# First modulation group in two parts: shift and scale ahead of the first sublayer, its gate third in gated jobs 3 to 10

## The reference

```python
def sublayer_input(x, g, mod_j):
    shift, scale, gate = mod_j[:, 0], mod_j[:, 1], mod_j[:, 2]
    h = rmsnorm(x, g) * (1 + scale[:, None, :]) + shift[:, None, :]
    return h, (1 + gate)[:, None, :]

def swiglu(h, w_gu, w_down):
    g, u = jnp.split(h @ w_gu, 2, axis=-1)
    return (jax.nn.silu(g) * u) @ w_down

    c_act = jax.nn.silu(c)
        mod = (c_act @ mod_w[layer] + mod_b[layer]).reshape(B, N_SUB, 3, D_MODEL)
        h, g = sublayer_input(x, norm_g[layer, 0], mod[:, 0])
        x = x + MACARON_W * g * swiglu(h, ffn_w_gu[layer, 0], ffn_w_down[layer, 0])
```

## Time and profile before

| | |
|---|---|
| median of 3 runs | 2380.91 us (2377.79 to 2382.84) |
| profiled execution | 2378.58 us |
| its span | 2377.0 us |
| granted TensorE clock, mean | 0.962 of full speed |
| PE busy | 2221.3 us, 93% |
| DVE busy | 1644.3 us, 69% |
| ACT busy | 1218.7 us, 51% |
| POOL busy | 327.2 us, 14% |
| DMA, mean | 224 GB/s |

### The profile page before, as it was taken

The page is one execution under the profiler, slowest core; times in us unless marked ns, Lnnn a source line. Parts: engine busy times, 40 slices in busy tenths (PEclk is TensorE's granted clock), DMA queues, the critical chain, the costliest instruction groups (busy, mean ns, idle before and its releaser), DMA issues.

```text
span 2377.0 us, 37520 instructions
## 1 busy us (share of the span) xinstructions
PE 2221.3 (93%) x14452; PEld 2031.1 (85%) x14452; DVE 1644.3 (69%) x1961; ACT 1218.7 (51%) x1911; POOL 327.2 (14%) x482
## 2 busy tenths in 40 slices
PE   2999999999999996999998999998998799998998
PEld 2998887998899795899886998987987798877987
DVE  6767764767776776776787776796766776665654
ACT  2544445544554465653464554556545554575543
POOL 0111000111121103021101120400210221000210
PEclk9999999999999998999999999999999899999999
DMA  8788883698897872797765678513788378442553
GB/s 335 249 300 292 273 295 109 239 315 288 262 322 258 310 220 72 225 324 266 259 225 189 197 262 287 174 53 99 256 288 246 91 269 282 148 135 71 180 201 106
DMA packets 296577, 532.97 MB, mean 224 GB/s; under 512 B 10097, under 2 KB 187644, under 8 KB 296444
## 3 DMA queue, kind: packets, MB, share of 16 engines
q1 hardware_dynamic: 263452, 358.05, 46.2%
q0 software_dynamic: 32992, 173.09, 20.4%
HBM read 530.00 MB, written 1.11 MB: 223 GB/s over the span
## 4 chain that ended last, share of the span: by engine, by line
PE 82%; DVE 7%; ACT 5%; issue 3%; DMA 3%; SPq 0%; POOL 0%; DVEq 0%; ACTq 0%
PE bk L1362 12%; PE bk L1363 12%; PE bk L1364 12%; PE bk L1261 9%; PE bk L1263 9%; PE bk L1262 8%; PE bk L1413 3%; PE bk L1616 2%; PE bk L1306 2%; DVE w_lo L1744 2%; DMA mod_raw<-in_ada_w 1%; PE bk L1249 1%; PE bk L1251 1%; PE bk L1250 1%; DVE mod_acc L1763 1%
## 5 line engine op out<-in xcount | busy, mean ns | idle before, releaser
L1744 DVE TENSOR_TENSOR w_lo<-raw,w_hi 128x1024 fp32r<-128x1024 f32 (+5 forms) x720 | 833.4, 1186 | 489.6 <-ACT w_hi L806 487.6
L806 ACT ACTIVATE w_hi<-raw 128x1024 fp32r<-128x1024 f32 (+5 forms) x720 | 683.3, 976 | 676.1 <-PE bk L1263 340.2
L1362 PE MATMUL bk<-a_hi,w_hi 128*128 128x256 f32 x2332 | 664.5, 285 | 5.9 <-DVE a_lo L1829 5.9
L1363 PE MATMUL bk<-a_lo,w_hi 128*128 128x256 f32 x2332 | 662.9, 284 | 0.0
L1364 PE MATMUL bk<-a_hi,w_lo 128*128 128x256 f32 x2332 | 662.8, 284 | 0.0
L1362 PEld LDWEIGHTS bk<-a_hi,w_hi 128*128 128x128 f32 x2332 | 451.0, 193 | 7.1 <-DVE a_lo L1829 4.5
L1363 PEld LDWEIGHTS bk<-a_lo,w_hi 128*128 128x128 f32 x2332 | 450.8, 193 | 0.0
L1364 PEld LDWEIGHTS bk<-a_hi,w_lo 128*128 128x128 f32 x2332 | 450.5, 193 | 0.0
L1763 DVE SCALAR_TENSOR_TENSOR mod_acc<-mod_raw,cact,mod_acc 128x1536 f32<-128x1536 f32 x182 | 329.7, 1811 | 38.1 <-DMA mod_raw<-in_ada_w 22.5
L1261 PE MATMUL bk<-w_hi,hid_hi 128*128 128x512 f32 x832 | 324.4, 390 | 3.3 <-DVE w_lo L1744 3.2
L1263 PE MATMUL bk<-w_hi,hid_lo 128*128 128x512 f32 x832 | 327.3, 393 | 0.0
(11 more groups left out here) (345 smaller groups left out, 3136.0 us busy)
## 6 DMA issues: line engine op xcount, KB each, us to landing
raw<-in_ffn_w SPq DMA_DIRECT2D x128, 1024.0 KB, 5.6
mod_raw<-in_ada_w POOLq DMA_DIRECT2D x128, 768.0 KB, 6.3
raw<-in_ffn_w_gu SPq DMA_DIRECT2D x88, 1024.0 KB, 7.4
mod_raw<-in_mod_w POOLq DMA_DIRECT2D x80, 768.0 KB, 7.0
raw<-in_ffn_w_down SPq DMA_DIRECT2D x40, 1024.0 KB, 7.1
first_mod<-in_mod_w SPq DMA_DIRECT2D x16, 768.0 KB, 9.8
raw<-in_sb_w_qkv SPq DMA_DIRECT2D x12, 1024.0 KB, 8.7
raw<-in_conv_w_pw SPq DMA_DIRECT2D x12, 1024.0 KB, 5.5
```

Source lines behind the costliest of these rows:

```text
L806: ins = act.activation(o(w_hi[:, p % OPS, :]), r(raw[:, c % RAWS, :]), ACT.Copy)
L1362: pe.matmul(o, wh, a_hi[:, f, :], start=(f == 0), stop=False)
L1363: pe.matmul(o, wh, a_lo[:, f, :], start=False, stop=False)
L1744: ins = dve.tensor_tensor(o(w_lo[:, p % OPS, :]), r(raw[:, c % RAWS, :]), o(w_hi[:, p % OPS, :].bitcast(F32)), ALU.subtract)
```

## The change

The modulation of the first sublayer is computed in two parts.

- Units of group 0 are now 128 x 1024 (512 KB): first eight of shift, then eight of scale. SP issues them first of all, behind two small transfers of c, with x between the second and the third. The parameter rows go to POOL's queue.
- c is turned by itself, and its Silu no longer waits for the parameter rows. ACT's statistics of x, DVE's normalised tokens and PE's turning of x (`turn_x`) stand before the sum. PE sums 16 columns, not 24, in two parts of eight (`part_sum`), with ten filling matmuls (`keep_busy`) before the second.
- The gate third is loaded by POOL, 8 blocks of 512 KB (`gate_load`), two of them in job 9's place, and added by DVE in jobs 3 to 10 (`gate_add`). PE sums it ahead of job 11, for which it waits for `gate_made` 8. DVE finishes it after the second unit of group 2 in the projection, and POOL writes it out and reads it back there.
- Group 1's first unit is issued only when all 16 units of group 0 are added.
- The rope angles, lambda's softplus and the Sin move to the second sublayer.

```diff
-FIRSTS = 7
+FIRSTS = 10
...
+        def gate_out_of(w):
+            return bk[:, 4 * (w % 2) + 3, 0:KD]
+        GATE_JOBS = (3, 4, 5, 6, 7, 8, 9, 10)
...
+            for h, name in enumerate(("c", "c_2")):
+                sp.dma_start(crow[h * KD:h * KD + KD, :], as_rows(t[name])).then_inc(c_landed, 16)
             for u in range(UNITS):
+                if u == 2:
+                    sp.dma_start(x[:, :, :], t["x"][0].rearrange("(b p) d -> p b d", p=P)).then_inc(x_landed, 16)
                 if u >= FIRSTS:
                     sp.wait_ge(mod_used, 2 + u - FIRSTS + 1)
                 w, at = mod_of(0)
-                sp.dma_start(first_mod[:, u % FIRSTS, :], w[u // 2 * P:u // 2 * P + P, at + u % 2 * MODW:at + (u % 2 + 1) * MODW])\
+                sp.dma_start(first_mod[:, u % FIRSTS, :], w[u % KD * P:u % KD * P + P, at + u // KD * D:at + (u // KD + 1) * D])\
                     .then_inc(first_landed[u % FIRSTS], 16)
...
+            def gate_load(j):
+                if j >= 2:
+                    pool.wait_ge(gate_made, j - 1)
+                w, at = mod_of(0)
+                pool.dma_start(gate_raw[j % 2][:, :], w[j * P:j * P + P, at + 2 * D:at + 3 * D]).then_inc(gate_landed[j % 2], 16)
...
+            pool.wait_ge(mod_used, 2 + UNITS)
+            mod_load(1, 0)
...
+                    if st["n"] == 0:
+                        for j in range(KD):
+                            mod_next(g, j + 1)
+                            if j in (2, 3):
+                                gate_load(j - 2)
+                            hid_low(n + j, j, j % 2)
+                            if j >= 4:
+                                gate_load(j - 2)
+                    else:
+                        mod_rest(g, lambda i, b: hid_low(n + 2 * i + b, 2 * i + b, b))
                     for b in range(3):
                         if b:
                             mod_next(g + 1, b)
                         hid_low(n + 8 + b, 8 + b, b % 2)
-                    gate_tile(st["n"])
+                        if st["n"] + b == 0:
+                            gate_load(6)
+                            gate_load(7)
+                    if st["n"]:
+                        gate_tile(st["n"])
...
                     for r in range(3, KD):
                         mod_next(g + 1, r)
+                        if st["n"] == 0 and r == 3:
+                            pool.wait_ge(gate_ready, 1)
+                            gate_row(0)
+                            gate_tile(0)
...
+            act.preload_act_table(ACT.Silu)
+            act.wait_ge(c_turned, 1)
+            act.activation(cact[:, :], bk[:, 7, 0:2 * KD], ACT.Silu).then_inc(cact_ready, 1)
+            act.preload_act_table_set("natural_log_exp_and_others")
             act.wait_ge(consts, 1)
-            act.wait_ge(turn_read, 1)
-            act.activation(cact[:, 0:KD], col("c", 0, KD), ACT.Silu)
-            act.activation(cact[:, KD:2 * KD], col("c_2", 0, KD), ACT.Silu)
-            act.activation(lsp[:, 0, :], col("lru_lambda", 0, NB), ACT.Abs).then_inc(cact_ready, 1)
-            act.wait_ge(cact_ready, 1)
-            act.activation(lsp[:, 1, :], lsp[:, 0, :], ACT.Exp, scale=-1.0).then_inc(cact_ready, 1)
+            act.wait_ge(x_landed, 16)
+            for b in range(2):
+                square(xt[:, b, :], x[:, b, :], b)
+                tokens_inverse(b, 22 + b)
...
+            pe.wait_ge(c_landed, 32)
+            pe.transpose(bk[:, 7, 0:2 * KD], crow[:, :], ident[0:2 * KD, 0:2 * KD]).then_inc(c_turned, 1)
...
+            def part_sum(acc, out):
+                for j in range(KD):
+                    ins = pe.matmul(out[:, j:j + 1], acc[:, P * j:P * j + P], one1[:, 0:1], start=True, stop=True)
+                return ins
+            is_free(pe, 0)
+            pe.wait_ge(mod_used, 2 + KD)
+            part_sum(mod_acc[:, 0:D], mod_out(0)[:, 0:KD])
+            pe.wait_ge(loaded, 16 * NLOADS)
+            for j in range(NPT):
+                n = min(P, NROW - P * j)
+                ins = pe.transpose(job_flat(0, 2048)[:, D + P * j:D + P * j + n], rows[0:n, j, :], ident[0:n, 0:n])
+            ins.then_inc(turn_done, 1)
+            k.add("turn", 1)
+            pe.wait_ge(cact_ready, 1)
             pe.wait_ge(rope_read, 1)
+            turn_x(0)
+            pe.wait_ge(mod_used, 2 + UNITS - 2)
+            keep_busy(job_banks(0)[:, 0, :], 10)
+            pe.wait_ge(mod_used, 2 + UNITS)
+            part_sum(mod_acc[:, D:2 * D], mod_out(0)[:, KD:2 * KD]).then_inc(turn_done, 1)
...
+                    if g == 0:
+                        is_free(pe, w + 11)
+                        pe.wait_ge(gate_made, KD)
+                        part_sum(gate_acc, gate_out_of(w + 11)).then_inc(gate_summed, 1)
...
+            dve.wait_ge(cact_ready, 1)
+            for r in range(4):
+                mod_add(0, r, 0)
             dve.wait_ge(rope_in, 1)
-            own_wait(own(dve.tensor_copy(rcol[:, :], bk[:, 0, 0:2])))
...
-            mod_finish(0, 0)
+            own_wait(own(dve.tensor_copy(rcol[:, :], bk[:, 6, 0:2])))
+            dve.tensor_scalar(rs[:, 0, :], bk[:, 6, S:2 * S], rcol[:, 0:1], None, ALU.mult).then_inc(rope_read, 1)
+            for r in range(4, KD):
+                mod_add(0, r, 0)
+            for r in range(3):
+                mod_add(0, r, 1)
+            tokens_normed(0)
+            for r in range(3, 6):
+                mod_add(0, r, 1)
+            dve.wait_ge(turn_done, k.next("turn") + 1)
...
+            def gate_add(j):
+                dve.wait_ge(gate_landed[j % 2], 16 * (j // 2 + 1))
+                if j == 0:
+                    dve.tensor_scalar(gate_acc[:, :], gate_raw[0][:, :], cact[:, 0:1], None, ALU.mult).then_inc(gate_made, 1)
+                else:
+                    dve.wait_ge(gate_made, j)
+                    dve.scalar_tensor_tensor(out=gate_acc[:, :], in0=gate_raw[j % 2][:, :], scalar=cact[:, j:j + 1], in1=gate_acc[:, :],
+                                             op0=ALU.mult, op1=ALU.add).then_inc(gate_made, 1)
...
+                            if g == 0 and 2 * i + b in GATE_JOBS:
+                                gate_add(GATE_JOBS.index(2 * i + b))
...
+                        if g == 0:
+                            gate_add(GATE_JOBS.index(b))
...
+                            if g + m == 0 and u == 1:
+                                dve.wait_ge(gate_summed, 1)
+                                own_wait(own(dve.tensor_tensor(mv[:, 0, 16:24], gate_out_of(w + 11), mod_bias(0)[:, 16:24], ALU.add)))
+                                dve.tensor_scalar(mv_g[:, 0, :], mv[:, 0, 16:24], 1.0, 0.5, ALU.add, ALU.mult).then_inc(gate_ready, 1)
...
+                    rope_angles()
                     for m in range(HEADS // 2 + 3):
                         heads_out(2 * (m - 3), 6)
+                        if m == 2:
+                            lambdas()
```

More of the change, by code:

```diff
@@ L949, in _ @@
                 if after(g) == "first":
-                    act.wait_ge(x_landed, 16)
-                    for b in range(2):
-                        square(xt[:, b, :], x[:, b, :], b)
-                        tokens_inverse(b, 22 + b)
                     pieces(p + 2, p + 4)
-                    act.wait_ge(rope_arg, 1)
-                    act.activation(rope[NOPE:P, :], rs[NOPE:P, 0, :], ACT.Sin).then_inc(rope_ready, 1)
                 elif after(g) == "final":
@@ L1174, in _ @@
                         heads_out(2 * (m - 3), 6)
+                    act.wait_ge(rope_arg, 1)
+                    act.activation(rope[NOPE:P, :], rs[NOPE:P, 0, :], ACT.Sin).then_inc(rope_ready, 1)
                     pieces(p + 28, p + 31)
@@ L1423, in _ @@
             pe.wait_ge(consts, 1)
-            pe.wait_ge(loaded, 16 * NLOADS)
-            turn(0, [rows[0:min(P, NROW - P * j), j, :] for j in range(NPT)])
-            turned()
+            pe.wait_ge(c_landed, 32)
+            pe.transpose(bk[:, 7, 0:2 * KD], crow[:, :], ident[0:2 * KD, 0:2 * KD]).then_inc(c_turned, 1)
             pe.wait_ge(pos_ready, 1)
@@ L1813, in a_values @@
                 w = stages[g]["w"]
-                tokens_normed(g)
+                if g:
+                    tokens_normed(g)
                 if stages[g]["late"]:
@@ L1950, in _ @@
+            pieces(0, 2)
+            dve.wait_ge(turn_done, k.next("turn") + 1)
+            dve.tensor_tensor(mv[:, 0, 0:16], mod_out(0)[:, 0:16], mod_bias(0)[:, 0:16], ALU.add).then_inc(turn_read, 1)
+            dve.wait_ge(turn_read, k.get("turn"))
+            dve.scalar_tensor_tensor(out=mv_a[:, 0, :], in0=mv[:, 0, 8:16], scalar=1.0, in1=col("norm_g", 0, 8),
+                                     op0=ALU.add, op1=ALU.mult).then_inc(mod_ready, 1)
             for st in stages:
```

148 lines of the change are left out of this document (83 added, 65 removed).

## The result

| | before | after |
|---|---|---|
| median | 2377.92 us (8 runs) | 2386.65 us (8 runs, 2380.13 to 2389.66) |
| ratio | | 1.0040, 95% interval 1.0027 to 1.0054 |
| profiled execution, span | 2378.58, 2377.0 us | 2380.13, 2378.5 us |
| granted clock, mean | 0.962 | 0.957 |

The change makes the kernel slower by 0.4%, some 9 us. The forecast was 4 us faster (2376.9); the result lies inside its range of 2364 to 2389, on the side to which it gave 0.18.

What follows compares the result with a forecast made beforehand. PE's starts and waits were taken as the bound; -25.8 + 0.2 (lambda, angles, Sin) + 3.6 + 11.8 + 6.2 = -4.0 us, giving a median of 2376.9 us, range 2364 to 2389 for 8 in 10.

Steps and rivals of the forecast that it cites:

- What bounds the kernel: Whole kernel: PE has 82% of the span; it ends earlier only if PE starts earlier or waits less.
- Part 1: Start: loading only shift and scale before job 0 starts PE 27.3 us sooner; gain 25.8 net of low clock.
- rival (b): Start: POOL's two blocks go ahead of the second weight chunk, PE starts 3.5 later; net -0.5, 2380 us; chance 0.15.
- the bound without delay: Start: upper bound of Part 1's gain, 27.5 us, if the second weight chunk is not delayed.
- Part 2: Gated jobs 3 to 10: gate adds use up the ACT and DVE ring's lead, then stop PE; cost 3.6 us.
- Rival (a): Gated jobs have more room: part 2 costs 0, part 3 8.2, part 4 3.0; net -14.6, 2366 us; chance 0.2.
- Part 3: Before the output projection: PE waits for the eighth gate product, then sums at lower clock; cost 11.8 us.
- Part 4: Projection: POOL waits for the gate row's write, delaying modulation loads, DVE and PE; cost 6.2 us, bounds 3 to 9.
- three pieces of 2.8: Projection: PE work of three pieces, 2.8 us each, with w_lo already made, behind the delayed modulation product.
- (c): Gated jobs: POOL's queue sets the pace, five jobs lose 1.7 each; net +5.6, 2387 us; chance 0.15.

Runs made afterwards that it cites:

- row_apart: Changed kernel with five more modulation loads issued between the write of the gate's row and its read-back; 2386.2 us, 1.0035 to the kernel before.
- both: Changed kernel with the edits of row_apart and add_first together; 2370.8 us, 0.9975 to the kernel before.
- read_only: As both, with the gate row's write left out and the tile read from the bias in memory; 2369.2 us, 0.9968 to the kernel before.
- ones_tile: As add_first, but no row written or read: PE makes the gate's tile from gate_acc with a matrix of -1; 2365.8 us, 0.9937 to the kernel before.
- add_first: Changed kernel with the eighth gate product at the beginning of job 10 instead of its end; 2375.1 us, 0.9985 to the kernel before.
- before_row_late: Kernel before, with only the gate row's write and read-back moved into the projection; 2388.8 us, 1.0054 to the kernel before.
- one_gate: As both, with only one of the eight gate blocks loaded and added; 2369.2 us, 0.9969 to the kernel before.

## Why the prediction was wrong, point by point

**What bounds the kernel.** Right in the main: what PE wins or loses at the start, in its waits and in its clock adds up to the 6.8 us by which the next sum is later.

**Part 1, gain 25.8.** Job 0's first product came at 38.9, not 37.7 us: 26.3 us sooner, where 27.3 were worked out. The second weight chunk was converted from 36.36 us on; 3.0 behind the first, as in a free stretch, so rival (b) did not come about; its two blocks were asked for only at 34.7 us, as DVE had finished the sixteenth unit, and not at 31. Two errors nearly cancel here: the last block landed at 30.2 and the first chunk at 33.25 us, 2 us later than worked out, but the second chunk was not delayed. (By its own terms the prediction should have had DVE's units end at 31.0, the second chunk land at 35.4 and PE start at 38.0, and the bound without delay be 26.6, not 27.5; that changes little.) Whether queues share by packets or by bytes this case doesn't tell. The low clock cost at most about 1.7 (1.5 taken): 98.7 us from job 0 to the sum before, 100.4 with one add only. Gain net of it 24.6. Lambda, angles and Sin cost nothing that shows: PE's waits from 270 to 425 us are the same list, the one for sb_s 2.4 us before and 2.1 after.

**Part 2, cost 3.6.** The mechanism was right, the size a little short: 4.1 us (the 5.8 of the table less 1.7). The clock of the sum in job 8 adds 1.8 by two traces each, of which before's own two differ by 2.8. Rival (a), that the adds are hidden, fell.

**Part 3, cost 11.8.** Right in kind, and near in size: the wait was 6.3 and 6.4 us (5.5 + 2.0 taken, but DVE's wait for a load in job 9 was 0.5 and 0.7, not 2.0), the sum 3.54 (3.5). With the 10.5 us in the table and 2.3 for the low clock that reaches into the projection (0.43 us a product until 197.4, 0.23 from then on) it comes to 12.8. Moving the last product ahead of the job gave 12.4 back.

**Part 4, cost 6.2.** This is the step that failed: the term for the write and read of the gate's row measured 12.5 us (the projection loses 14.8, of which 2.3 belong to part 3), twice what was taken and beyond its bound of 9. The chain in the changed kernel is the one forecast: POOL idle behind the write, the next block late, DVE without it, PE without w_lo, then about 5.4 us at the low clock, 2.7 lost (2.5 taken). What was wrong is the length of PE's wait, 9.7 and 10.6 us where 3 to 4 were worked out. Of these 6 us the write accounts for some 4: it took 9.9 and 10.8 us, not 6. I had gone under the median of 8.7 in the earlier trace rows since "while modulation loads are held the engines are half free"; they were (a share of 0.32 from 216 to 222 us), and the write was no faster. The block then took 8.1 and not 7, and the work that PE still had while DVE stood still was 7.1 us, not three pieces of 2.8.

The experiments add what the sum could not have: POOL's wait is only one of the write's two costs. Where POOL doesn't wait for it (row_apart, both), the blocks in flight beside the write land in 13.1 to 14.8 us instead of 7, so the projection still takes 75.4 and 69.6 us; where the row isn't written (read_only, ones_tile) it takes 62.3 and 63.1, against 61.3 before. From add_first's 73.5 to read_only's 62.3 the wait is 3.9 us and the slow blocks are 7.3. That is why moving the wait away gained 1.3 us in row_apart, and why before_row_late loses as much in a kernel with no other change. With 12.5 in place of 6.2 the forecast's sum gives +2.3 and, with 24.6 for the start and 4.1 for the adds, +4.0 us; the clock in job 8's sum makes it 5.8, and 12.8 for part 3 6.8, which is the place of the next sum.

**The rivals.** (c), slower, gave 2387 and so the right time, by luck: its mechanism did not come, there is no wait of DVE for a load in the gated jobs but one of 0.52 us in job 9. (a), more room in the jobs, is refuted by one_gate and by the waits of 6.3 and 9.7 us.

**What stays open.** The first sublayer accounts for 6.8 of 9 to 10 us. The mean clock over all runs is 0.9525 in after and 0.9603 in before (32 runs), but that is nearly all the first sublayer's own: the traces show 41 us at 0.50 in it after and 7 before, which leaves by the same estimate 186 us behind it against 182, worth 1 to 2 us. The last 1 to 2 us are not accounted for. What sets the low time in stages that are the same in both kernels was not found; one_gate and read_only have 12 to 14 us more of it than both.

## What to carry to other kernels

A transfer is priced by its pieces as well as its bytes, and by what it does to the others: a row written element by element took 10 to 20 us here and made the blocks beside it land 5 to 8 us later. It may stand only where nobody wants these blocks, as it did at the start of the old kernel. To hide the issuing engine's wait for it is not enough. A step that was free where it stood must be priced anew, with its neighbours, where it is moved to. And a product whose result another engine waits for belongs ahead of its job's other work: one line's place gave 12 us here.

## What was not expected of the hardware

- A 4 KB write of 4-byte pieces in the projection landed in 9.9 to 13.2 us from POOL's queue and in 19.5 from ACT's; blocks of 768 KB beside it, issued behind it, in another queue or 0.5 us ahead, took 12.5 to 14.8 us. Its own packets filled 1.6% of the engines' time in the 40 us around it.
- A sum over partitions by a 128 x 128 matrix of -1 takes two products of 512 columns, 1.88 us, and leaves its result in every partition: no slower than the 16 records of one column (1.84) that give it in one.
- Two POOL operations a job lengthened DVE's modulation products by a quarter.
